# Weights of two neighbouring output tiles laid out column by column in turn, and read with a step of two

## The reference

```python
h = h + hybrid_mixer(rmsnorm(h, norm_mix), w_in, ...)        # attention and short convolution
h = h + swiglu(rmsnorm(h, norm_ffn), w_gate, w_up, w_down)   # hidden width 5632
...
h = x @ w_in_2                                               # q, k, v, pooled branch, two gates
merged = sigmoid(gate_attn) * y_attn + sigmoid(gate_pool) * y_pool
x = layer_norm(ALPHA * x + merged @ w_out_2)
f = square(relu(x @ w_ff1)) @ w_ff2                          # hidden width 8192
x = layer_norm(ALPHA * x + f)
```

## Time and profile before

| | |
|---|---|
| median of 2 runs | 2449.69 us |
| the profiled execution's own time | 2449.89 us |
| its span, from the first to the last instruction | 2447.8 us |
| TensorE matmul busy | 2433.8 us, 99% |
| TensorE weight loads busy (beside matmuls) | 2173.7 us, 89% |
| VectorE, ScalarE, GpSimd busy | 1614.5, 1202.2, 173.9 us |
| read from memory | 445.12 MB, 183 GB/s over the span |

### The profile page before, as it was taken

One profiled execution on the slowest core, in us unless ns is written; L12 is line 12 of the kernel. 1 busy time (PEld: TensorE's weight loads), 2 busy tenths in 40 slices (PEclk: granted clock), 3 DMA queues, 4 the chain that ended last, 5 costly groups with the idle time before them and its releaser, 6 DMA issues.

```text
span 2447.8 us, 36417 instructions
## 1 busy us (share of the span) xinstructions
PE 2433.8 (99%) x14762; PEld 2173.7 (89%) x14762; DVE 1614.5 (66%) x2518; ACT 1202.2 (49%) x1728; POOL 173.9 (7%) x195
## 2 busy tenths in 40 slices
PE   8999999999999999999999999999999999999999
PEld 8999998888888888888888888888998888888887
DVE  5646676676666666667677756678885665565667
ACT  6545545544544543455555654544554443443544
POOL 0001111000000000002211102031110000000010
PEclk9999999999999999999999999999999999999999
DMA  7554456666566666665655455565566666656663
GB/s 250 180 161 139 141 165 189 200 184 194 182 198 190 189 190 189 192 190 185 197 188 167 166 185 190 184 193 186 162 196 193 189 189 189 194 190 189 183 193 117
DMA packets 125751, 449.59 MB, mean 184 GB/s; under 512 B 13840, under 2 KB 16400, under 8 KB 125584
## 3 DMA queue, kind: packets, MB, share of 16 engines
q1 hardware_dynamic: 125296, 446.91, 58.8%
q10 hardware_dynamic: 288, 0.36, 0.0%
HBM read 445.12 MB, written 2.10 MB: 183 GB/s over the span
## 4 chain that ended last, share of the span: by engine, by line
PE 96%; DVE 2%; ACT 1%; issue 0%; DMA 0%; ACTq 0%
PE out_bank L614 28%; PE out_bank L618 27%; PE out_bank L615 14%; PE out_bank L617 14%; PE out_bank L622 3%; PE out_bank L621 3%; PE out_bank L623 3%; DVE w_lo L1307 1%; ACT w_hi L895 0%; PE side_bank L734 0%; PE side_bank L694 0%; PE side_bank L749 0%; PE side_bank L725 0%; DVE h L1824 0%; DMA h<-in_tokens 0%
## 5 line engine op out<-in xcount | busy, mean ns | idle before, releaser
L1307 DVE TENSOR_TENSOR w_lo<-raw,w_hi 128x1024 fp32r<-128x1024 f32 x839 | 1037.4, 1240 | 601.0 <-ACT w_hi L895 596.9
L895 ACT CAST w_hi<-raw 128x1024 fp32r<-128x1024 f32 x840 | 878.1, 1049 | 953.6 <-PE out_bank L618 874.8
L614 PE MATMUL out_bank<-a_op,w_hi 128*128 128x512 f32 x1984 | 784.2, 395 | 0.5 <-DVE h L1334 0.3
L618 PE MATMUL out_bank<-a_op,w_hi 128*128 128x512 f32 x1984 | 776.7, 391 | 0.0
L615 PE MATMUL out_bank<-a_op,w_lo 128*128 128x256 f32 x1984 | 558.8, 282 | 0.0
L617 PE MATMUL out_bank<-a_op,w_lo 128*128 128x256 f32 x1984 | 552.0, 278 | 0.0
L617 PEld LDWEIGHTS out_bank<-a_op,w_lo 128*128 128x128 f32 x1984 | 380.1, 192 | 84.3
L615 PEld LDWEIGHTS out_bank<-a_op,w_lo 128*128 128x128 f32 x1984 | 372.9, 188 | 77.0
L614 PE MATMUL out_bank<-b_op,w_hi 128*128 128x512 f32 x992 | 389.7, 393 | 0.0
L618 PE MATMUL out_bank<-b_op,w_hi 128*128 128x512 f32 x992 | 388.0, 391 | 0.0
L614 PEld LDWEIGHTS out_bank<-a_op,w_hi 128*128 128x128 f32 x1984 | 373.1, 188 | 2.0 <-DVE w_lo L1307 0.7
(11 more groups left out here) (302 smaller groups left out, 1974.6 us busy)
## 6 DMA issues: line engine op xcount, KB each, us to landing
raw<-in_w_ff SPq DMA_DIRECT2D x256, 512.0 KB, 4.2
raw<-in_w_in SPq DMA_DIRECT2D x223, 512.0 KB, 3.7
raw<-in_w_gu SPq DMA_DIRECT2D x176, 512.0 KB, 4.2
raw<-in_w_down SPq DMA_DIRECT2D x88, 512.0 KB, 4.3
raw<-in_w_out SPq DMA_DIRECT2D x64, 512.0 KB, 4.3
raw<-in_w_ba SPq DMA_DIRECT2D x16, 512.0 KB, 3.9
raw<-in_w_bp SPq DMA_DIRECT2D x16, 512.0 KB, 3.8
out<-h SPq DMA_DIRECT2D x8, 256.0 KB, 2.3
```

The source lines that it names most:

```text
L614: t_.e.matmul(bank[:, :], wh, a_both, start=start, stop=False, skip_group_check=True)
L618: mm = t_.e.matmul(bank[:, :], wh, a_both, start=False, stop=stop, skip_group_check=True)
L895: a.e.copy(w_hi[:, m % SPLIT, :], raw[:, u % RAW, :]).then_inc(hi_split)
L1307: v_.e.tensor_tensor(w_lo[:, m % SPLIT, :], raw[:, u % RAW, :], w_hi[:, m % SPLIT, :].bitcast(F32), ALU.subtract).then_inc(lo_split)
```

## The change

`pack_weight` lays the columns of two neighbouring output tiles in turn: column 0 of tile 0, column 0 of tile 1, column 1 of tile 0, and so on for 256 columns, then the same for tiles 2 and 3. A new function `stationary` picks a tile's 128 columns out of `w_hi` or `w_lo` with a step of two elements (8 bytes). `first_unit` and `product_step` use it. Each matmul has the same numbers as before, in the same order; no instruction of any engine is added, removed or moved, and the forget and pool pieces stay as they were.

```diff
+            def stationary(buf, slot, i, x):
+
+                at = i * BLOCK * P + x // 2 * 2 * P + x % 2
+                return buf[:, slot, at:at + 2 * P - x % 2:2]
+
...
-                        at = kt * BLOCK * P + x * P
                         to = bank_of(tile)[:, 0:TOK]
-                        wh, wl = w_hi[:, 0, at:at + P], w_lo[:, 0, at:at + P]
+                        wh, wl = stationary(w_hi, 0, kt, x), stationary(w_lo, 0, kt, x)
...
-                width = len(blk.tiles) * P
...
-                        at = i * width + x * P
-                        wh, wl = w_hi[:, slot, at:at + P], w_lo[:, slot, at:at + P]
+                        wh, wl = stationary(w_hi, slot, i, x), stationary(w_lo, slot, i, x)
...
     m = m.reshape(rows // (UNIT_K * P), UNIT_K, P, cols // (BLOCK * P), BLOCK * P)
+    m = m.reshape(m.shape[:4] + (BLOCK // 2, 2, P)).swapaxes(-1, -2).reshape(m.shape)
     m = m.transpose(3, 0, 2, 1, 4)
```

## The result

The changed kernel takes 2494.86 us (median of 2 runs, 2494.83 to 2494.90) against 2449.69 us: 45 us or 1.85% longer, ratio 1.0185 with a 95% interval of 1.0155 to 1.0214. The forecast was 2465; the measured time lies in its range, but the price is three times the forecast's 15 us. The new lines are L616, L617, L619, L620 for the pair form (L614, L615, L617, L618 before) and L623 to L625 for the other.

The account below looks back on a forecast made before the run. TensorE's matmuls, busy 99%, bound the kernel by how closely they follow one another. 12 us behind L617 and 3 us under 258 columns make +15: 2449.9 + 15 = 2464.9, said as 2465, range 2446 to 2600.

Parts of the forecast that it names:

- (a): Host lays columns of two tiles in turn; transfers' bytes and the splits on ScalarE and VectorE stay: cost 0.
- (b): No instruction, wait or queue entry moves on any engine; forget and pool weights are read as before.
- +8 ns per load: Stationary loads with step 2: 1024 bytes passed over at 8.9 per ns take 115 ns, period 0.118 to 0.119 us.
- Rival 1: Stationary loads: the step is free, +0, 2450 us; chance 0.34 together with the rival of disturbed writers.
- under 512 columns nothing: Loads beside 512-column matmuls: a period of 0.119 us stays hidden under a cover of 0.230, so no cost.
- behind the second short one: Distance behind L617, 256 columns: 0.115 becomes 0.119 us, 2976 x 4 ns = 12 us.
- behind the first short one: Distance behind L615, 256 columns: 0.119 us already, so cost 0.
- the other form: Matmuls of 272 and 258 columns: nothing under 272, 2 ns for each of 1536 under 258, 3 us.
- upper end of +66 us: Short covers already bound by the load's end: each of the 8232 pays all 8 ns, +66 us.
- Rival 2: Short covers: each element a fetch of its own, load period 0.110 to 0.217 us, +812, 3262 us; chance 0.22.
- rival 3: Wider load reads disturb ScalarE, VectorE and transfers: less than +5 us, 2450 to 2455; chance 0.34 together with the free step.
- long covers stretch as well: Sign that the forecast is wrong in kind: 512-column matmuls also lengthen, the read of the moving side being disturbed.

Follow-up runs that it names:

- e8: Changed kernel (step 2) with moving rows 264 apart from element 48, both operands in one shared buffer behind w_lo: 2452.11 us.
- m2_cycles: TensorE alone repeats the kernel's cycle of four for all 16 ways of step 1 or 2: all packed 693.5 ns, all with the step 708.5.
- e4: Kernel before, packed loads, with moving rows 260 elements apart in place of 258: 2482.68 us, ratio 1.0131.
- e11: Changed kernel (step 2, rows of 258) with the first element of the moving rows at 40 in place of 48: 2471.99 us.
- e7: Kernel before, packed loads, with moving rows 264 apart from element 32: 2454.67 us, ratio 1.0021.
- e10: Kernel before, packed loads, rows of 258, first element of the moving rows moved from 48 to 56: 2489.18 us.
- m4_places: TensorE alone, first elements of loads and moving rows moved; rows of 264 from element 32: 706.5 ns a cycle with the step, 695.2 packed.
- m3_rows: TensorE alone, cycle of four with rows 256 to 272 apart, loads packed, step 2, misaligned or shorter: 693.3 to 713.3 ns for packed and step 2.
- m1_streams: TensorE alone, 48 matmuls of one kind behind one another: with 512 columns most frequently 227 ns packed, 233 with step 2.

## Why the prediction was right or wrong

- **What bounds the kernel** (TensorE's matmuls one behind another; the other engines have room): right. TensorE alone gives both cycles, and the splits and transfers stayed as they were.
- **Part (a) and (b), cost 0**: right.
- **"+8 ns per load", from the bytes passed over at 8.9 per ns**: nearly right in size, for a reason that holds only up to a step of 4. The recorded duration went from 188 to 196 ns, the bare period from 112 to 118 ns, and steps 3 and 4 followed the same line to 175 and 233 ns. Step 8 left it (238 ns in place of some 460), so what counts is not the bytes passed over but, as far as the five steps tell, the 16-byte pieces that are touched. Rival 1, the free step, is wrong as a rule of the load. The Trainium skill's note (SBUF — State Buffer, "Door 1: The DMA port swizzle") puts the free step at up to four float32; the measurement decides against it, since step 4 makes the load twice as long and the kernel 1.41 times. The two accesses to a line that the Trainium skill asks for in the same note fit these runs better: with two, at step 2, the load takes 118 ns in place of 112, with fewer 175 (step 3) and 233 (step 4).
- **"under 512 columns nothing"**: this is the step that failed. Behind the long matmuls the distance grew by 4.7 and 5.6 ns, which is 30 us where the sum had 0. The other terms came out: behind the second short one (L617 before) 4.7 ns, 14 us for 12; behind the first short one -0.3 ns, -1 us for 0; the other form +2.4 us for 3. Together it is 15 ns a cycle in place of 4. I had treated each distance as the greater of a cover and a load, which are fixed lengths. The runs show that the four together take a length that jumps, 693, 700, 707 or 713 ns, with the places of the operands, and that the kernel before stood at the least of them. The step threw it off. So the two terms that came out are no proof of their working either: in e8, with the step and the old cycle time, the four distances (mean of the cycles that follow one another) are 228, 117, 118 and 232 ns where the kernel before has 231, 119, 115 and 229. The mean over 24 places puts 7 of the 45 us to the step itself, which can't be told from zero; the rest is the lost place.
- **My support for it was an accident.** That 256 columns take half of what 512 take, 0.115 and 0.230, I read as the moving side's own pace. It is the good place's: with TensorE alone 512 columns stood from 227 to 233 ns apart, and 256 from 113 to 120, with packed loads alone.
- **The upper end of +66 us** held the result, but by a sum (every short cover pays all 8 ns) that did not happen: the short covers paid 5 ns at one of two places, and those of 258 and 272 columns next to nothing.
- **Rival 2** (the load halves its pace) did not come with step 2 (it did with step 4, 233 ns), and rival 3 (the writers disturbed) is out by m2_cycles. The last sentence of the prediction had named the sign: "long covers stretch as well". It had only no mechanism and no share of the chances.

What makes the grid is not shown. The distances between regular values, 6.67 ns, are 16 cycles of 2.4 GHz, and which length a cycle takes depends on the first byte and the row distance of the moving operand and on the start, step and number of columns of the loads. Whether the readers of the moving and of the stationary operand meet in the memory, or each waits for a turn of its own, no run here tells, and no run tells a good place from a bad one ahead of time.

## What to carry to other kernels

Where matmuls with loads of their own follow one another without a gap, read the length of the repeating group from the starts, divide the sum of its columns by the clock (here 1536 columns, 640 ns), and look how much lies above: 53 ns here at best, 80 at worst. A change of a few ns to any load or operand there can move the group by 7 to 27 ns (693 to 720 here), so try it in two or three places of its operands before judging it. Short streams of the group on TensorE alone, dozens of places in one run, gave five of the eight kernels e4 to e11 within 2.5 us and all of them within 10. For e4 to e7 that was read only afterwards; e8 to e11 were foretold, three of them within 2.5 us and e10 within 10.

## What the runs showed of the hardware that I had not expected

- Four matmuls of 512, 256, 256 and 512 float32r columns with packed loads took 693.3 to 720.0 ns a cycle by the place of their operands alone; the worst was rows of 258 from element 52 (m4_places).
- A shorter load is not a cheaper one: 64 columns in place of 128 made the cycle 706.7 in place of 693.3 ns (m3_rows).
- A load of 128 float32r columns takes 112 ns with step 1, 118 with 2, 175 with 3 and 233 with 4 (m2_cycles), and 238 with 8 (m1_streams, clock at 0.5): the rise ends at step 4, where each element has 16 bytes to itself.
- A load with step 4 takes 233 ns at either level of the clock (m1_streams at 0.5, m2_cycles at 1.0), so this pace is not set by TensorE's clock.
